# Three Strassen sets per feed-forward unit instead of two, with sums that move from PSUM bank to PSUM bank

## What is computed

```python
def swiglu(x, w_gate, w_up, w_down):
    return (jax.nn.silu(x @ w_gate) * (x @ w_up)) @ w_down
...
x = x + rms_norm(swiglu(hn, ...), ...)             # first block, layers 0 and 1
x = x + _swiglu(_rmsnorm(x, norm_ffn[i]), ...)     # second block, layers 0 and 1
```

## Time and profile before

| | us |
|---|---|
| median of 3 runs (1228.41 to 1228.79) | 1228.73 |
| the profiled execution's own time | 1228.27 |
| its span in the trace | 1226.4 |
| TensorE busy | 1219.6 |
| VectorE busy | 1013.4 |
| ScalarE busy | 751.4 |

### The profile page before, as it was taken

One profiled execution on the slowest core, in us unless ns is written; L12 is line 12 of the kernel. 1 busy time (PEld: TensorE's weight loads), 2 busy tenths in 40 slices (PEclk: granted clock), 3 DMA queues, 4 the chain that ended last, 5 costly groups with the idle time before them and its releaser, 6 DMA issues.

```text
span 1226.4 us, 16404 instructions
## 1 busy us (share of the span) xinstructions
PE 1219.6 (99%) x6284; PEld 1013.5 (83%) x6284; DVE 1013.4 (83%) x1436; ACT 751.4 (61%) x1154; POOL 97.9 (8%) x123
## 2 busy tenths in 40 slices
PE   9999999999999999999999999999999999999998
PEld 7778888888888888888888888888888888888887
DVE  8986999889788798878887756988888785989787
ACT  8875756555998655555687536465556643745552
POOL 2520000000100100000232000000001300000000
PEclk9999999999999999999999999999999999999999
DMA  8544455546654564645555234556455315464552
GB/s 342 154 142 138 173 207 187 206 172 206 205 195 169 187 206 172 237 174 206 198 187 172 69 104 145 203 178 230 172 206 190 133 35 206 173 211 166 206 189 86
DMA packets 32830, 218.75 MB, mean 178 GB/s; under 512 B 3936, under 2 KB 4576, under 8 KB 7408
## 3 DMA queue, kind: packets, MB, share of 16 engines
q1 hardware_dynamic: 30384, 210.32, 48.8%
q0 software_dynamic: 1648, 6.88, 2.2%
q10 hardware_dynamic: 720, 0.50, 0.1%
HBM read 216.64 MB, written 1.05 MB: 177 GB/s over the span
## 4 chain that ended last, share of the span: by engine, by line
PE 94%; DVE 4%; issue 1%; ACT 1%; DMA 0%; SPq 0%; DVEq 0%; ACTq 0%
PE PS L521 26%; PE PS L523 26%; PE PS L522 26%; PE PS L527 6%; PE PS L1022 2%; PE PS L1046 1%; PE PS L558 1%; PE PS L630 1%; PE PS L624 1%; PE PS L625 1%; PE PS L556 1%; PE PS L555 1%; DVE WL L2050 1%; DMA RAW<-in_w 0%; PE PS L963 0%
## 5 line engine op out<-in xcount | busy, mean ns | idle before, releaser
L2050 DVE TENSOR_TENSOR WL<-RAW,WH 128x2048 fp32r<-128x2048 f32 (+3 forms) x198 | 420.8, 2131 | 97.8 <-ACT WH L1364 97.8
L1364 ACT ACTIVATE WH<-RAW 128x2048 fp32r<-128x2048 f32 (+3 forms) x200 | 356.6, 1789 | 119.2 <-PE PS L523 119.1
L521 PE MATMUL PS<-WH,HTh 128*128 128x512 f32 (+1 forms) x752 | 296.9, 395 | 0.1
L523 PE MATMUL PS<-WH,HTl 128*128 128x512 f32 (+1 forms) x752 | 291.6, 388 | 0.0
L522 PE MATMUL PS<-WL,HTh 128*128 128x512 f32 (+1 forms) x752 | 291.3, 387 | 0.0
L523 PEld LDWEIGHTS PS<-WH,HTl 128*128 128x128 f32 x752 | 141.2, 188 | 29.4
L521 PEld LDWEIGHTS PS<-WH,HTh 128*128 128x128 f32 x752 | 141.3, 188 | 29.3 <-DVE WL L2050 1.1
L522 PEld LDWEIGHTS PS<-WL,HTh 128*128 128x128 f32 x752 | 141.4, 188 | 26.9
L521 PE MATMUL PS<-WH,YAh 128*128 128x512 f32 x354 | 139.9, 395 | 0.1
L523 PE MATMUL PS<-WH,YAl 128*128 128x512 f32 x354 | 138.0, 390 | 0.0
L522 PE MATMUL PS<-WL,YAh 128*128 128x512 f32 x354 | 137.8, 389 | 0.0
(11 more groups left out here) (546 smaller groups left out, 2051.0 us busy)
## 6 DMA issues: line engine op xcount, KB each, us to landing
RAW<-in_w SPq DMA_DIRECT2D x196, 1024.0 KB, 4.9
WL<-in_w POOLq DMA_DIRECT2D x2, 1024.0 KB, 9.0
BC<-in_rows POOLq DMA_DIRECT2D x4, 512.0 KB, 4.1
YG<-in_mem POOLq DMA_DIRECT2D x4, 512.0 KB, 4.9
X<-in_x SPq DMA_DIRECT2D x2, 512.0 KB, 5.4
RAW<-in_w SPq DMA_DIRECT2D x4, 256.0 KB, 5.7
BC<-in_s SPq DMA_DIRECT2D x1, 512.0 KB, 11.3
YG<-in_s SPq DMA_DIRECT2D x1, 512.0 KB, 9.2
```

The costliest lines, as they stand in the source:

```text
L521: e.matmul(out, ah, bh, start=start, stop=False, skip_group_check=joined)
L523: return e.matmul(out, al, bh, start=False, stop=stop, skip_group_check=joined)
L1364: e.activation(WH[:, c % NW, w], RAW[:, c % NR, w], ACT.Copy).then_inc(S.hi, 1)
L2050: e.tensor_tensor(WL[:, c % NW, w], RAW[:, c % NR, w], WH[:, c % NW, w].bitcast(f32), SUB).then_inc(S.lo, 1)
```

## The change

`SETS` becomes (3, 6, 9): three pairs of groups per unit are worked in sets. In a set the first two chunks (k tiles 0 to 3) are now one fast product of depth two (`set_mm`), and the third and fourth are plain and add onto the same banks. Sums are no longer added up behind the set: C11's first product is copied by ScalarE into C22's bank (`cu`) and accumulated upon; the product in C12's bank is saved (`c7`); VectorE joins both into C21's bank (`j1`); C22 goes to C12's bank (`cv`) and VectorE adds the saved one to C22 (`j2`). The sums of weights are made in two steps: `set_hi`/`set_ahead` before the set, `late_hi`/`late_raw` in it, when TensorE has used the first (`qt`). Their rounded forms lie in the free first quarter of WH and in YB. The third chunk's split is made in two halves (`half_of`, `half_rest`, semaphore `n1h`, `n1l`). Folds have banks of their own (`FOLD_BANK`) and come in pairs between the two chunks of a group, one in each set, and 9 and 10 behind the second down chunk. The steps of `decay_rates` (small ones of the RG-LRU's constants) move on VectorE from the first unit into the stage behind it. The core of the diff (TensorE's set, the three orders, ScalarE's `column_set` and VectorE's):

```diff
-SETS = (2, 6)
+SETS = (3, 6, 9)
 NS = 2 * len(SETS)
-BANKS = ((0, 1), (6, 7), (0, 2), (1, 3), (6, 7), (2, 3), (0, 2), (1, 3), (6, 7), (0, 1), (6, 7))
+BANKS = ((0, 1), (6, 7), (4, 5), (0, 2), (1, 3), (6, 7), (2, 4), (3, 5), (0, 1), (6, 4), (7, 5))
+FOLD_BANK = (0, 6, 7, 0, 1, 6, 2, 3, 0, 6, 4)
...
+                rests_ready(e, cs[0])
+                bank_free(C11)
+                add(C11, Y(0, 0, 0), W(0, 1), start=True)
+                rests_ready(e, cs[1])
+                add(C11, Y(1, 0, 0), W(1, 1), stop=True).then_inc(S.qa, 1)
+                e.wait_ge(S.gsl, 2 * f + 2)
+                bank_free(C12)
+                add(C12, sum_of(0, 2), T(0, 0, 1), start=True).then_inc(S.qt, 1)
+                add(C12, sum_of(1, 2), T(1, 0, 3), stop=True).then_inc(S.qt, 1)
+                e.wait_ge(S.cu, n + 1)
+                add(C22, sum_of(0, 1), T(0, 1, 2)).then_inc(S.qt, 1)
+                add(C22, sum_of(1, 1), T(1, 1, 4)).then_inc(S.qt, 1)
+                add(C11, Y(0, 1, 0), W(0, 2))
+                add(C11, Y(1, 1, 0), W(1, 2))
+                e.wait_ge(S.j1, n + 1)
+                add(C22, sum_of(0, 0), T(0, 0, 5))
+                add(C22, sum_of(1, 0), T(1, 0, 6)).then_inc(S.qc, 1)
+                e.wait_ge(S.n1l, n + 1)
+                for t, b in enumerate((C11, C21)):
+                    for k in (4, 5):
+                        rows(cs[2], k, t, 0, b)
+                e.wait_ge(S.cv, n + 1)
+                add(C12, sum_of(0, 3), W(0, 3)).then_inc(S.used, 1)
+                add(C12, sum_of(1, 3), W(1, 3)).then_inc(S.used, 1)
+                add(C21, Y(0, 1, 1), T(0, 1, 7))
+                add(C21, Y(1, 1, 1), T(1, 1, 8))
+                e.wait_ge(S.j2, n + 1)
+                rests_ready(e, cs[2])
+                for t, b in enumerate((C12, C22)):
+                    for k in (4, 5):
+                        tk = rows(cs[2], k, t, 1, b)
                 tk.then_inc(S.used, 1)
                 folds()
+                rests_ready(e, cs[3])
+                for t in range(2):
+                    for k in (6, 7):
+                        for half in range(2):
...
-                fold(0)
-                set_mm(f, 2, cs[4:8], lambda: fold(1))
-                group(4)
-                fold(2)
-                fold(3)
-                group(5)
-                fold(4)
+                group(2, lambda: two_folds(0))
+                set_mm(f, 3, cs[6:10], lambda: fold(2))
+                group(5, lambda: two_folds(3))
                 set_mm(f, 6, cs[12:16], lambda: fold(5))
-                group(8)
-                fold(6)
-                fold(7)
-                group(9)
-                fold(8)
-                group(10)
-                fold(9)
-                wide_mm(cs[22:], ed + 1, lambda k: ydst(f, k), lambda ci: e.wait_ge(S.ylo, fold_n(f, 9 if ci == FAST[0] else ci)), lambda: fold(10), 1, f)
+                group(8, lambda: two_folds(6))
+                set_mm(f, 9, cs[18:22], lambda: fold(8))
+                e.wait_ge(S.ylo, fold_n(f, 8))
+                wide_mm(cs[22:], ed + 1, lambda k: ydst(f, k), lambda ci: e.wait_ge(S.ylo, fold_n(f, 9 if ci == FAST[0] else ci)), lambda: two_folds(9), 1, f)
...
+                def column_set(a, *folds):
+                    n = set_n(f, a)
+                    C11, C12, C22 = BANKS[a][0], *BANKS[a + 1]
+                    half_of(cs[2 * a - 1], 0)
+                    e.wait_ge(S.qa, n + 1)
+                    if a > SETS[0]:
+                        e.wait_ge(S.an, gt_n(f, [g for g in range(a) if C22 in BANKS[g]][-1], 1))
+                    copy(PS[:, C22, :], PS[:, C11, :]).then_inc(S.cu, 1)
+                    half_of(cs[2 * a - 1], 1)
+                    e.wait_ge(S.qt, 4 * n + 2)
+                    copy(FB[f][5][:, 3, :], PS[:, C12, :]).then_inc(S.c7, 1)
+                    late_hi(a, 0, 0)
+                    late_hi(a, 1, 0)
+                    tanh(a - 1)
+                    e.wait_ge(S.qc, n + 1)
+                    copy(PS[:, C12, :], PS[:, C22, :]).then_inc(S.cv, 1)
+                    late_hi(a, 0, 1)
+                    late_hi(a, 1, 1)
                     feed(cs[2 * a])
+                    feed(cs[2 * a + 1])
+                    for g in folds:
+                        fold(g)
...
+                feed(cs[3])
                 fold(0)
-                sums_hi(cs[5])
-                feed(cs[3])
-                column_set(2)
-                group(4, 2, 3)
+                fold(1)
+                set_hi(3, 0)
+                feed(cs[4])
+                set_hi(3, 1)
+                column_set(3, 2)
+                set_hi(6, 0)
+                fold(3)
+                fold(4)
                 feed(cs[10])
-                sums_hi(cs[13])
-                tanh(5)
-                kept(4)
-                feed(cs[11])
-                fold(4, True)
-                column_set(6)
-                group(8, 6, 7)
-                group(9, 8)
-                group(10, 9)
+                set_hi(6, 1)
+                column_set(6, 5)
+                set_hi(9, 0)
+                fold(6)
+                fold(7)
+                feed(cs[16])
+                set_hi(9, 1)
+                column_set(9, 8)
                 if f < 3:
                     e.activation(st[:, 60:62], mh[:, 0:2], ACT.Exp)
-                wide_mm(cs[22:], ed + 1, lambda: fold(10), at=1, f=f)
+                wide_mm(cs[22:], ed + 1, lambda: two_folds(9), at=1, f=f)
...
+                def column_set(a, *folds):
+                    n = set_n(f, a)
+                    C21, C22, M7 = BANKS[a][1], BANKS[a + 1][1], FB[f][5][:, 3, :]
+                    late_raw(a, 0, 0)
+                    late_raw(a, 0, 1)
+                    late_raw(a, 1, 0)
+                    half_rest(cs[2 * a - 1], 0)
+                    set_rest(a, 5, 0, 0)
+                    e.wait_ge(S.c7, n + 1)
+                    e.wait_ge(S.qt, 4 * n + 4)
+                    e.tensor_tensor(PS[:, C21, :], PS[:, C22, :], M7, ADD).then_inc(S.j1, 1)
+                    set_rest(a, 6, 1, 0)
+                    late_raw(a, 1, 1)
+                    half_rest(cs[2 * a - 1], 1)
+                    gate(a - 1)
+                    e.wait_ge(S.cv, n + 1)
+                    e.tensor_tensor(PS[:, C22, :], PS[:, C22, :], M7, ADD).then_inc(S.j2, 1)
+                    set_rest(a, 7, 0, 1)
+                    set_rest(a, 8, 1, 1)
                     feed(cs[2 * a])
...
-                    e.wait_ge(S.tr, 4 * FASTS[c - NR] + 4)
+                    m = FASTS[c - NR]
+                    e.wait_ge(S.tr, 4 * m + (4 if m % len(FAST_AT) >= NS or m % 2 else 6))
```

356 lines of the change are left out of this document (181 added, 175 removed).

## The result

The changed kernel takes **1272.33 us** (median of 4 runs, 1272.17 to 1273.36) against 1228.57 for the kernel before on the same chip (4 runs): ratio 1.0358, 95% interval 1.034 to 1.0376. Slower by 43.8 us, inside the forecast's range; forecast 1269. Of all executions told of here one stands apart, one of the four of e4_head, with 3603.88 us against 1267.3 to 1267.5 for the other three; its kernel's median moves by less than 0.1 with it.

What follows compares the result with a forecast made beforehand. TensorE bounds the kernel: number of matmuls times their pace. 1228.3 - 5.4 - 0.6 + 47.6 (four units of 1.6+4.6+3.7+2.0 = 11.9) = 1269.9, stated as 1269 us; range 1248 to 1281, chance 0.80.

Steps and rivals of the forecast that it cites:

- What it removes: TensorE over four units: 24 fewer 512-column matmuls, -5.4 us, and seven clumps of fold transposes for nine, -0.6 us.
- The decay-rate steps: Small steps moved on VectorE from the first unit to the stage behind: 0, at most +1 us.
- rival A: The saving comes through: set inputs ready early, fold 9 not waited for, only -6.0 stays, 1222 us; chance 0.05.
- Fold 9: Behind the second down chunk TensorE waits for fold 9's remainder: 2.0 us per unit, ends 1.3 and 2.3.
- Head of a set: One chain over ScalarE and VectorE to the join; TensorE goes on at L+6.9 against 5.44, losing L + 1.5 us.
- L: Moment, from the set's first matmul, when VectorE ends the second chunk's split: 0.15 (set 3), 2.2 (set 9), 3.1 (set 6).
- Set 3, 9, 6: Losses per unit of 1.6, 3.7 and 4.6 us; in sets 9 and 6 the split stands behind a fast fold.
- The bank copy: ScalarE's copy of 512 columns from bank to bank: taken as 0.60 us; at 1.05, 5 us more in all.
- that cover is gone: Before, split and sums preceded fold 4, so ScalarE's 3.65 us stand before a fast fold's copy cost nothing.
- B: Only the hand-overs cost, everything else being early: 10 us less 6.0, 1233 us; chance 0.10, with anything up to 1245.
- C: The clock falls to 1.2 GHz after each of eight long losses, 2 us each on top: 1285 us; chance 0.05.
- D: No new set at all; excluded by the count of 24 fewer matmuls, no chance given.

Runs made afterwards that it cites:

- e4_head: Changed kernel with the bank copy, first late sum and C12's saving ahead of the third chunk's half splits on ScalarE, the join earlier on VectorE: 1267.47 us.
- e3_fold9: Changed kernel with fold 9 in bank 7 instead of 6, so the first fast down chunk's first product no longer waits for its remainder: 1264.24 us.
- e11_between: Changed kernel with the second chunk's split ahead of sets 6 and 9 moved between the fast fold's first step and its rounding: 1261.81 us.
- e8_split_between: As e5, but the split of the set's fourth chunk stands between the late fast fold's first step and its rounding: 1238.04 us.
- e2_folds_in: Changed kernel with fold 4 (set 6) and folds 6 and 7 (set 9) moved from before the set to behind its last late sum: 1266.50 us.
- e5: Changed kernel with the edits of e2_folds_in, e3_fold9 and e4_head together: 1265.61 us.
- e1_split_first: Changed kernel with the second chunk's split and its two sums ahead of the pair of folds, before sets 6 and 9, on ScalarE and VectorE: 1279.43 us.
- e9_warm: e2_folds_in plus ten unused 512-column matmuls on TensorE behind the transposes of folds 9 and 10: 1261.70 us.

## Why the prediction was right, point by point

In short: the mechanism was the forecast one at each of its places. The sets were priced right (9.9 us per unit forecast, 9.8 measured, of which 9.6 at the joins), fold 9 too (8.0 and 8.2 in all). Two small terms were not: the clumps (0.6 forecast, nothing found) and the moved decay-rate steps (0, at most 1 forecast; 2.1 found).

**What it removes**: the 24 matmuls, 5.4 us. The further 0.6 for fewer clumps is not borne out: a pair costs 0.90 and a lone fold 0.46 in the kernel before, so joining two folds saves next to nothing.

**The decay-rate steps**: "0, at most +1", because VectorE was busy 128 of 156 us there. It was 2.1 us, at one point of that stage where TensorE had 0.9 us to spare. This is the occupancy argument that the prediction refuses under rival A, used once by itself.

**Fold 9**, 2.0 per unit (1.3 to 2.3): 2.0 in all four, 8.1 with e3_fold9. The reason was also the named one, VectorE's chunk remainders first.

**Head of a set**, L + 1.5: the join was passed 4.54 us late in set 6, where the rule gives 4.6 with L = 3.06; 3.50 in set 9 with L = 2.0 (2.2 forecast), rule 3.5; 1.57 in set 3 with L = 0.1 (0.15), rule 1.6. The chain itself was exact (join passed at zero + 9.99 against L + 6.9 = 10.0). What the table has more, about 0.35 per set, is the 0.15 of its reckoning and 0.2 behind the join, of which 0.11 are the second matmul after the wait, which comes 0.33 to 0.34 after the first instead of 0.227. Earlier waits of a set add nothing by this, since the join comes at its own time.

That L + 6.9 came out to a few hundredths is partly luck. The prediction runs the chain over ScalarE's late copy, at L + 5.5. But VectorE never waits for that copy; its own row has no gap from L to the join, in set 6 from 497.52 to 504.47, and is just as long. e4_head showed it: with ScalarE's part 1.05 us shorter, sets 3 and 9 gained 0.45.

**Set 3, 9, 6** by L: 1.6, 3.7, 4.6 forecast, 1.9, 3.9, 4.9 in the table and 1.6, 3.5, 4.5 at the join; the order of the three and its cause (a split behind a fast fold) hold. **The bank copy**, bound between 0.60 and 1.05, took 0.58.

**What I had not seen**: "small errors of order in L go rather down" put the forecast at 1269 where its own sum gave 1270 (1269.9 for the profiled execution), and the terms left out went up; "some 50" entries were forecast for TensorE's list of waits, and 34 new ones and that of the stage behind the first unit are there; "TensorE busy falls by 6 us" was wrong, it rose by 13. The claim that the kernel before was covered by its own interleaving ("that cover is gone") is what e11_between and e8_split_between restored, for 10.5 us outside the set and 27.6 inside. The bound "L cannot be under 0.9" holds only for that order: e2 went below.

**Rivals.** A (the saving comes through) fell. The Trainium skill ("Perfetto Trace Analysis", Identifying the Most-Contended Engine) takes the occupancy of VectorE and ScalarE as a fair measure of how close they are to their limit; read as room for more work it failed here, where VectorE at 81% and ScalarE at 62% went with 3.6% more time. The room is real, 34 of 44 us came back without removing any work, but only by order. B (hand-overs only, 1233) is what e8 nears with 1238. C (the clock, 1285): the mechanism was real and its price was not. It fell four times, not eight, and each time in the shadow of a later wait (e3_fold9); uncovered it costs 1.5 us (e2_folds_in), not 2. The Trainium skill ("TensorE: Matmul & The Clock Gate", HAM oscillation) has idle gaps sending the clock to half; the traces agree for gaps of 2.3 us, though not for each of them, and the changed kernel's shows none for 1.24 (clock 1.00 in set 9). D was excluded rightly.

## What to carry to other kernels

When a step of one engine waits for another engine in its middle, put independent work that both need soon *between* its halves; a fold kept whole in front of a split cost 27.6 us here against the same work interleaved (e5 and e8, the clock's falls included), 10.5 us in another place (the change and e11). Price a change that makes the fastest engine wait by the whole of what stands in each engine's order between the releasing and the wanted step: in e1 reordering inside that stretch gave nothing, in e11 its idle time could be won. And a gain measured alone (0.45 a set) may be smaller than the wait removed, since the next engine or the clock stands right behind. Small steps that are moved out of the way need the same look: nine of 0.2 us went with 1.5 us more where they came to stand.

## What was not expected of the hardware

- Behind every wait of TensorE the next matmul comes 0.33 to 0.34 us after the first, against 0.227 in a run without waits: 0.11 us, which adds to the time only behind the last wait of a chain.
- The clock fell to half for some 3 us behind waits of 2.0 to 3.6 us, but not behind each: in e1_split_first the wait of 3.61 us in set 6 of unit 1 left it at 1.00, the same wait in units 0, 2 and 3 did not. It also fell behind one wait of 1.46 us (e11_between, unit 0), and behind none of those of 1.75 us. What decides it stays open.
- Ten matmuls for nothing in such a gap made the kernel 4.8 us faster (e9_warm).
- ScalarE copies 512 columns from PSUM bank to PSUM bank in 0.58 us, no dearer than to SBUF (0.60).
